# One decoder step on one core: the first layer opens with the input, and the memory tiles move between the samples' memory steps

## The reference

```python
# memory keys and values of both layers, from 256 rows
mem_n = rmsnorm(mem_prompt, mem_norm[l])
mem_k_p[l], mem_v_p[l] = mem_n @ w_mem_k[l], mem_n @ w_mem_v[l]      # 256 columns each
# layer 0
z = rmsnorm(h, a_norm1) @ a_w_in        # 1024 -> 6 heads x 128 of q, k, v, gate, and 256 of memory queries
q, k = rope(z_q), rope(z_k)
s_new, o = retention(state, q, k, v)
mix = head_groupnorm(o) * silu(g)
om = mem_attend(qm, mem_k[0], mem_v[0]) # the samples read their own cached keys and values
h = h + concat(mix, om) @ a_w_out
# then an MLP; layer 1 (latent attention, memory attention, MLP); a final norm
```

## Time and profile before

| | |
|---|---|
| median of 3 runs | 1627.74 us (1625.76 to 1630.88) |
| the profiled execution, its own time | 1629.53 us |
| its span, first to last instruction | 1627.7 us |
| TensorE busy | 1537.8 us, 94% of the span |
| VectorE, ScalarE, GpSimd busy | 821.3, 570.1, 50.4 us |
| mean granted TensorE clock | 0.978 |
| first tile of head 0 starts | 88.34 us |
| first tile of head 1 starts | 123.43 us |

### The profile page before, as it was taken

One profiled execution on the slowest core, in us unless ns is written; L12 is line 12 of the kernel. 1 busy time (PEld: TensorE's weight loads), 2 busy tenths in 40 slices (PEclk: granted clock), 3 DMA queues, 4 the chain that ended last, 5 costly groups with the idle time before them and its releaser, 6 DMA issues.

```text
span 1627.7 us, 28935 instructions
## 1 busy us (share of the span) xinstructions
PE 1537.8 (94%) x11449; PEld 1425.3 (88%) x11449; DVE 821.3 (50%) x1290; ACT 570.1 (35%) x889; POOL 50.4 (3%) x76
## 2 busy tenths in 40 slices
PE   3899999979999999999988889999899999999998
PEld 2888888869999999999988556766899999999998
DVE  4847777655433434334575556665454334343344
ACT  4532333323322313223443246554343223131243
POOL 1120000020000000000001000000000000000000
PEclk8999999979999999999999989999999999999999
DMA  6543222333232322323233404542122223232221
GB/s 195 167 137 93 80 79 80 89 102 88 79 91 79 91 79 77 90 77 90 78 82 104 121 16 117 148 123 76 57 74 85 86 79 90 78 90 84 82 79 59
DMA packets 229384, 149.35 MB, mean 92 GB/s; under 512 B 11121, under 2 KB 222466, under 8 KB 229282
## 3 DMA queue, kind: packets, MB, share of 16 engines
q1 hardware_dynamic: 218802, 122.57, 26.2%
q0 software_dynamic: 6032, 20.28, 4.2%
q10 hardware_dynamic: 4448, 5.11, 1.0%
HBM read 140.26 MB, written 7.68 MB: 91 GB/s over the span
## 4 chain that ended last, share of the span: by engine, by line
PE 84%; DVE 9%; ACT 4%; issue 2%; DMA 1%; ACTq 0%; DVEq 0%; SPq 0%
PE ps L597 65%; PE ps L1118 3%; PE ps L1076 3%; DVE wl L1623 2%; PE ps L1145 2%; PE ps L1059 1%; PE ps L1022 1%; PE ps L1023 1%; DVE onorm L1796 1%; PE ps L979 1%; DVE rstd L1642 1%; DVE ml L1627 1%; PE ps L982 1%; ACT wh L1228 1%; DVE gn L1790 1%
## 5 line engine op out<-in xcount | busy, mean ns | idle before, releaser
L597 PE MATMUL ps<-mh,wh 128*128 128x288 f32 (+1 forms) x1424 | 326.2, 298 | 21.3 <-DVE wl L1623 16.9
L597 PE MATMUL ps<-xh,wh 128*128 128x288 f32 x1542 | 336.6, 300 | 8.9 <-DVE wl L1623 7.9
L597 PE MATMUL ps<-xh,wl 128*128 128x288 f32 x1542 | 330.0, 296 | 0.0
L597 PE MATMUL ps<-xl,wh 128*128 128x288 f32 x1542 | 329.9, 296 | 0.0
L597 PE MATMUL ps<-ml,wh 128*128 128x288 f32 (+1 forms) x1424 | 323.5, 296 | 0.0
L597 PE MATMUL ps<-mh,wl 128*128 128x288 f32 (+1 forms) x1424 | 323.5, 296 | 0.0
L1228 ACT ACTIVATE wh<-raw 128x1024 fp32r<-128x1024 f32 (+1 forms) x195 | 202.2, 1037 | 285.4 <-PE ps L597 263.5
L1623 DVE TENSOR_TENSOR wl<-raw,wh 128x1024 fp32r<-128x1024 f32 (+1 forms) x195 | 232.9, 1195 | 74.3 <-ACT wh L1228 72.9
L597 PEld LDWEIGHTS ps<-xh,wh 128*128 128x128 f32 x1542 | 247.9, 190 | 20.1 <-issue 10.1
L597 PEld LDWEIGHTS ps<-mh,wh 128*128 128x128 f32 x1424 | 237.9, 191 | 25.4 <-DVE wl L1623 17.7
L597 PEld LDWEIGHTS ps<-xh,wl 128*128 128x128 f32 x1542 | 249.0, 190 | 0.0
(11 more groups left out here) (299 smaller groups left out, 1310.1 us busy)
## 6 DMA issues: line engine op xcount, KB each, us to landing
raw<-in_w_up SPq DMA_DIRECT2D x64, 512.0 KB, 4.0
raw<-in_w_down SPq DMA_DIRECT2D x64, 512.0 KB, 3.6
pages<-in_cache_mla SPq DMA_DIRECT2D x128, 160.0 KB, 2.2
raw<-in_a_w_in SPq DMA_DIRECT2D x26, 512.0 KB, 3.8
memkc<-in_cache_mem_k POOLq DMA_DIRECT2D x16, 256.0 KB, 4.4
memvc<-in_cache_mem_v POOLq DMA_DIRECT2D x16, 256.0 KB, 5.5
raw<-in_a_w_out SPq DMA_DIRECT2D x8, 512.0 KB, 3.6
raw<-in_b_w_out SPq DMA_DIRECT2D x8, 512.0 KB, 3.7
```

The lines of the kernel that those rows point to most:

```text
L597: last = mm(ps[:, 2 * (m % 2) + c, 0:n], w[:, s, kk, :], x(kk, col, n), start=(kk == 0 and nth == 0), stop=(kk == final and nth == 2))
```

## The change

It touches the stretch from the first instruction to the start of head 1, and nothing behind it but numbers of semaphores.

- **Numbers.** The two memory query tiles become m = 0 and 1 (`M_Q`), the four of head 0 m = 2 to 5 (`M_Z0`), the eight memory tiles m = 6 to 13 (`M_MEM`). Heads 1 to 5 keep m = 14 and on.
- **Loads.** SyncE loads the identity, the gains and the ones, waits until the whole input is there, and then loads from m = 2. ScalarE's queue loads the input as before and now, behind it, the two query tiles' weights and the memory rows. GpSimd waits for the input, loads two rope tables, then the samples' caches once six K steps are split, and the other six tables once all memory K steps are split (`mem_lo`); the four stores of the memory rows go behind the first load of the retention state.
- **Sums of squares in row layout.** ScalarE squares the input rows as they come from memory, 128 x 1024 at a time, with `accum_out` (five instructions, and two for the memory rows). Root and reciprocal are then on one number per partition. VectorE scales the identity by them (`row_diagonals`, `memory_diagonals`), and a matmul of ones with that diagonal spreads them over the partitions (`row_scales`, five matmuls; `memory_scales`, two). The sums on VectorE (L1633), the 128 x 576 reciprocal and the 128 x 256 one go.
- **K step by K step.** `x_turn(kk)` turns one K step of the input (five matmuls) into banks 4 to 7 or 2 and 3, and ScalarE and VectorE split it straight out of PSUM. The copies into `res` are shared, even K steps by ScalarE and odd ones by VectorE. `query_step(j, kk)` is the part of query tile j that belongs to K step kk.
- **Memory tiles later.** The memory rows are turned among the last query steps, copied by ScalarE, and split during head 0's tiles. The eight tiles stand after head 0's, with the second half of the samples' memory attention between them.

The diff, cut to its core:

```diff
-M_MEM = 0
-M_Z = M_MEM + 4 * DEPTH
+M_Q = 0
+M_Z0 = M_Q + 2
+M_MEM = M_Z0 + 4
+M_Z = M_MEM + 4 * DEPTH - (M_MEM - M_Q)
...
+X_BANK = [4, 6, 2, 4, 6, 4, 6, 4]
+X_AFTER = {3: 0, 4: 1, 5: 3, 6: 4, 7: 5}
...
+            for dst, name in ((ident, "c_ident"), (gain, "gains"), (ones, "c_ones")):
+                sp.dma_start(dst[:, :], t[name]).then_inc(gain_in, 16)
+            wa = t["a_w_in"][0]
+            sp.wait_ge(x_in[RT], 16)
+            for part in range(4):
+                load(m_z(0, part), wcols(wa, RET_W * part))
...
-            pool.wait_ge(x_hi, KD)
+            pool.wait_ge(x_hi, KD - 2)
             sample_memory(0)
...
+            pool.wait_ge(mem_lo, DEPTH * KD)
+            for dst, name in ((kdec, "c_kdec"), (blkq, "c_blkq"), (blkv, "c_blkv"),
+                              (maskA, "c_maskA"), (maskS, "c_maskS"), (qdec, "c_qdec")):
...
+            def x_turn(kk):
+
+                b = X_BANK[kk]
+                if kk in X_AFTER:
+                    pe.wait_ge(x_lo, X_AFTER[kk] + 1)
+                for r in range(RT + 1):
+                    if kk == 0:
+                        pe.wait_ge(x_in[r], 16)
+                    if r < RT:
+                        last = pe.transpose(ps[:, b, P * r:P * r + P], xrow[:, r, P * kk:P * kk + P], ident[:, :])
+                    else:
+                        last = pe.transpose(ps[:, b + 1, 0:NS], xsrow[:, P * kk:P * kk + P], ident[0:NS, 0:NS])
                 last.then_inc(xT_ready, 1)
...
+            def row_scales():
+
+                pe.wait_ge(diag_ready, 1)
+                pe.wait_ge(gain_in, 16 * 3)
+                pe.wait_ge(x_lo, 7)
+                for r in range(RT):
+                    mm(ps[:, 6, P * r:P * r + P], ones[:, :], t1[:, P * r:P * r + P], start=True, stop=True)
...
+            for j in range(2):
+                act.dma_start(raw[:, M_Q + j, :, :], wcols(t["a_w_in"][0], 4 * RET_W + P * j)).then_inc(w_loaded[M_Q + j], 16)
+            for n in range(2):
+                act.dma_start(memrow[:, n, :], t["mem_prompt"][0, P * n:P * n + P, :]).then_inc(mem_in, 16)
+
+            def x_squares(r):
+
+                act.wait_ge(x_in[r], 16)
+                rows, src = (P, xrow[:, r, :]) if r < RT else (NS, xsrow[:, :])
+                do(f(scratch[0:rows, :], src, ACT.Square, accum_out=vec[0:rows, 48 + r:49 + r]))
...
+            def x_tail(kk):
+
+                if kk % 2 == 0:
+                    dve.wait_ge(res_act, kk // 2 + 1)
+                dve.wait_ge(x_hi, kk + 1)
+                tail(xl[:, kk, :], pair(X_BANK[kk]), G_A1 + kk, xh[:, kk, :], C[x_lo])
```

```diff
             sample_keys(0, 2)
             sample_keys(0, 3)
+            z_tile(0, 2)
             sample_scores(0, 0)
-            z_tile(0, 1)
-            sample_keys(0, 4)
-            sample_keys(0, 5)
+            z_tile(0, 3, keys_between(4))
             sample_turn(0, 0)
             sample_keys(0, 6)
             sample_keys(0, 7)
             sample_values(0, 0)
-            z_tile(0, 2)
+            memory_tile(0)
+            sample_back(0, 0)
+            memory_tile(1)
             sample_scores(0, 1)
-            sample_back(0, 0)
-            z_tile(0, 3, first_turn)
+            memory_tile(2)
+            sample_turn(0, 1)
+            memory_tile(3)
             sample_values(0, 1)
+            memory_tile(4)
+            sample_back(0, 1)
+            memory_tile(5)
+            kv_to_rows(0)
+            kv_to_rows(1)
+            memory_tile(6)
...
```

More of the change, by code:

```diff
@@ L504, in put @@
                 n_out[0] += 1
[L507 to L515, removed]
+            pool.wait_ge(x_in[RT], 16)
+            for dst, name in ((ropeC, "c_ropeC"), (ropeS, "c_ropeS")):
+                pool.dma_start(dst[:, :], t[name]).then_inc(consts_in, 16)
             def sample_memory(layer):
@@ new lines, in query_step @@
+            def query_step(j, kk):
+                if j and kk == 0:
+                    pe.wait_ge(x_lo, 3)
+                dense(M_Q + j, tiles(xh), tiles(xl), ready=(x_lo, lambda kk: kk + 1), part=range(kk, kk + 1))
+            def row_scales():
[4 more added lines that the diff above has]
+                    mm(ps[:, 6, P * r:P * r + P], ones[:, :], t1[:, P * r:P * r + P], start=True, stop=True)
+                mm(ps[:, 7, 0:NS], ones[0:NS, :], t1[0:NS, SEQ:ROWS], start=True, stop=True).then_inc(ss_ps, 1)
@@ new lines, in memory_scales, with memory_tile @@
+            def memory_scales():
+                pe.wait_ge(diag_ready, 2)
+                pe.wait_ge(memT_taken, 1)
+                for r in range(2):
+                    last = mm(ps[:, 4, P * r:P * r + P], ones[:, :], t2[:, P * r:P * r + P], start=True, stop=True)
+                last.then_inc(ss_ps, 1)
+            def memory_tile(j):
+                layer = j // 4
+                dense(M_MEM + j, lambda kk, col, n: mh[:, kk, NMEM * layer:NMEM * layer + n],
+                      lambda kk, col, n: ml[:, kk, NMEM * layer:NMEM * layer + n], n=NMEM,
+                      ready=(mem_lo, lambda kk: KD * layer + kk + 1))
@@ L650, in kv_to_rows @@
                 last.then_inc(kv_rows_ps, 1)
-            stats(2 * KD)
-            for j in range(2):
-                dense(M_Z + j, tiles(xh), tiles(xl), ready=(x_lo, lambda kk: kk + 1) if j == 0 else None)
-                for m in range(4 * j, 4 * j + 4):
-                    kv_to_rows(m)
             def unit_scores_a(u):
@@ L1363, in middle @@
                         if h == 0 and part == 0:
-                            sample_heads(0, 1)
+                            for m in range(4, 8):
+                                kv_to_rows(m)
+                            act.wait_ge(consts_in, 16 * 8)
                         if u is not None:
@@ L1838, in _ @@
-            z_tile(0, 2)
+            w_tail(M_MEM)
+            z_take(0, 2)
+            for kk in range(2, 6):
+                memory_tail(1, kk)
+            z_take(0, 3)
+            sample_norm(0, 0)
+            w_tail(M_MEM + 1)
+            memory_tail(1, 6)
+            memory_tail(1, 7)
+            memory_tile(0)
+            gate(0)
+            w_tail(M_MEM + 2)
+            sample_low(0, 0)
+            memory_tile(1)
             sample_max(0, 1)
-            sample_low(0, 0)
+            w_tail(M_MEM + 3)
```

429 lines of the change are left out of this document (288 added, 141 removed).

## The result

The changed kernel takes **1618.24 us** (median of 20 runs, 1614.65 to 1633.86), the kernel before 1629.08 us in its 20 (1625.76 to 1634.11). The ratio is 0.9939, 95% interval [0.9926, 0.9952]: faster by 0.6%, some 11 us. I had forecast 1608, range 1601 to 1617. The direction was right, the number was not: 19.9 us were to be saved and 11 were. (Of the 20 runs the slowest, 1633.86, had a mean granted clock of 0.933; the others ended by 1622.40 at 0.980 to 0.983.)

What follows compares the result with a forecast made beforehand. TensorE was taken as the bound, busy 94%, with 34.8 idle us ahead of head 0 to win. Head 1 effectively 19.9 us earlier gave 1629.53 - 19.9 = 1609.6, then 1608 for the runs' lower median; range 1601 to 1617.

Steps and rivals of the forecast that it cites:

- Nothing behind head 1 is changed: Everything after head 1's start was taken as unaltered, so the 19.9 us saved by then would stay.
- the rest of the program follows TensorE, us for us: Beyond the 34.8 idle us ahead of head 0, the time was taken to move exactly with TensorE.
- S: Moment when ScalarE may first split the input, after its DMA issues, table load and four squares: 14.9 us, between 11.0 and 16.0.
- one stall of 3.73: Among ScalarE's four new DMA issues, one held 3.73 us and the others 0.5 each, leaving ScalarE free at 8.6.
- S to the query steps: From ScalarE's first input split to TensorE's first query step, waiting for the first weight: 6.1 us.
- To head 0: Head 0's first tile starts at S + 25.3 = 40.2 us, where it was 88.34.
- Head 0 to head 1: Old stretch of 35.1 us plus eight memory tiles and smaller moved work: 62.5 us, head 1 at 102.7.
- The 1.6 for hand-offs: Between head 0 and head 1, 1.6 us added for ten more hand-offs between tiles and one wait.
- Rival A: Low clock holds through the query steps because TensorE waits for single K steps: 1619 us; 7%.
- The rule weighed there: Full clock does not engage for transposes; 41 turns would cost 0.09 us more each, about 1611 us; trace said to disagree.
- Rival B: VectorE holds the eight memory tiles at 4.40 us each, costing 12 us more: 1620 us; 7%.
- Rival C: Six late rope tables hold ScalarE and VectorE in head 1's first tile; each us past 106 costs one; 2%.
- Rival D: Later layers are paced by something fixed, such as DMA, so the time stays unchanged; 3%.

Runs made afterwards that it cites:

- e1: Changed kernel with 100 already-met TensorE waits (50 instructions) added between the MLP loops of layers 0 and 1; 1610.92 us, ratio 0.9885.
- e2: Changed kernel with 20 already-met TensorE waits (10 instructions) added between the MLP loops of layers 0 and 1; 1623.61 us, ratio 0.9958.
- e3: Kernel before the change with 80 already-met TensorE waits (40 instructions) added between the two layers' MLP loops; 1646.14 us, ratio 1.0094.
- e5: Changed kernel with already-met TensorE waits, 30 instructions ahead of layer 0's MLP and 20 ahead of layer 1's; 1618.41 us, ratio 0.9937.
- e6: Kernel before the change with 160 already-met TensorE waits (80 instructions) ahead of layer 1's MLP; 1635.82 us, ratio 1.0041.
- e11: Changed kernel, memory rows loaded by SyncE, one square later, 20 filler turns of the identity, 80 met waits in layer 0's retention; 1604.96 us, ratio 0.9838.
- e4: e1 with the memory rows' two loads issued by SyncE behind its first two weight tiles, not by ScalarE; 1607.21 us, ratio 0.9862.
- e9: Changed kernel with e1's 100 met waits moved to where TensorE idles 4.65 us in layer 1's attention; 1609.05 us, ratio 0.9866.

## Why the prediction was wrong, point by point

- **"Nothing behind head 1 is changed"** is the step that failed, and with it "the rest of the program follows TensorE, us for us". No instruction behind head 1 is another, but all of TensorE's stand 27 further on in its code, and the loop of layer 1's MLP came to lie on eight pieces instead of seven. That cost 8.5 us in the profiled execution. The size of the miss, 1617.74 less the 1609.6 of my sum, is 8.1. e1, e2, e3, e5 and e6 show that it is the place: each adds nothing but met waits to one of the two kernels, and pauses and packets come and go with where these put the loops and not with their number, in either loop, in either kernel.
- **S** (14.9, bounds 11.0 to 16.0) was 16.5, above my upper bound. The table load was 1.28 and the four squares 1.18 each, as said or less. What was mis-sized is the issues: ScalarE was free at 10.5, not 8.6. I gave one stall of 3.73 to four issues; the two pairs took 2.82 and 4.41. The DMA engines move 396 GB/s in the window from 4 to 6 us of this trace, and the queue that was held once was held again.
- **S to the query steps** (6.1): 6.3. **To head 0** (S + 25.3): S + 26.2. Together with S, head 0 came at 42.7 instead of 40.2.
- **Head 0 to head 1** (62.5): 60.1. The 1.6 for hand-offs was not needed; TensorE is busy 59.66 of the 60.14. The two errors cancel, and head 1 at 102.85 is right by luck as much as by working. 19.3 us ahead at split 17, where I had 19.9.
- **Rival A**, the low clock in the query steps: no. It lasted 2.8 us, from 22.8 to 25.6, and cost 1.4; I had 1.7 in the sum. **The rule weighed there**, of the Trainium skill (TensorE: Matmul & The Clock Gate, Part 4: PE-mode transpose), that turns do not bring the full clock: the turns of the earlier trace rows and e11's, at full clock from 18.8 us with only turns before, disagree with it.
- **Rival B**, memory tiles held by VectorE: no, TensorE did not wait. **Rival C**, late tables: no. Head 1's retention rows waited 0.82, for ScalarE's copy. **Rival D**, a gain that does not arrive: in its effect this is what happened to 8.5 of the 19.9, but not by its mechanism, DMA; the later layers are not paced by anything fixed, as e1, e4 and e9 show.
- The **range** took in every cost of the opening and none of the program's length. A row of the profile stood there for it, the instruction queue, and the changed kernel could be built and its loops' places counted before any run.

## What to carry to other kernels

A change is also a change of place for all code behind it. Where a kernel has a loop of some thousand instructions, count in each engine's compiled code how many pieces the loop touches before and after, and read the instruction queue's packets on the page: more packets without more instructions, and pauses ended by "issue" behind a jump, are code being fetched, and some tens of instructions of met waits in an idle spot ahead of the loop (50 in e9, 40 in e11) can take them away. Count before padding: 10 in e2 made it worse. And compare a change with another whose code is shifted harmlessly, before its gain is put down as what the idea is worth: 11 us here became some 20.

## What was not expected of the hardware

- A loop of 1579 instructions on TensorE is held from pass to pass when it touches seven pieces of 256 and fetched anew when it touches eight: 67 against 85 packets. A jump then costs some 2.7 us of standing still, up to 2 more where the edge of the next piece is near, and none to 6.8 us at half clock behind it, 3.6 to 7 us in all.
- TensorE's clock falls after it has restarted, 0.9 us later in the rows at 1393.45 and 0.1 us later at the second jump, so the cost of a pause stands in rows that look busy.
- A met wait costs TensorE 33 to 41 ns (3.32 us for 100, 6.55 for 160).
- The same 30 us near 860 run at a mean clock of 1.00 or 0.89 in kernels whose code is the same there and whose past differs, worth about 3 us. In these traces it is one reason why gains shown in the opening do not add to the us at the end. What decides it stays open.
